# Prompt attention: values of head pairs on two column halves, divided by spread reciprocals

## The reference, cut to what matters

```python
sc = jnp.einsum('bqhd,bqkhd->bqhk', q, kg).astype(jnp.float32) * (q.shape[-1] ** -0.5)
sc = jnp.where(valid[:, :, None, :], sc, -jnp.inf)
p = jax.nn.softmax(sc, axis=-1).astype(v.dtype)
return jnp.einsum('bqhk,bqkhd->bqhd', p, vg)
```

## Time and profile before

| | |
|---|---|
| median of three runs | 2633.05 us |
| the profiled execution | 2633.2 us, span 2631.5 us |
| busy PE / DVE / ACT / POOL | 2504.1 / 1316.3 / 986.7 / 510.4 us |
| prompt attention, first score to last value | 1267.21 to 1593.60 us of the span |

### The profile page before, as it was taken

One profiled execution on the slowest core, in us unless ns is written; L12 is line 12 of the kernel. 1 busy time (PEld: TensorE's weight loads), 2 busy tenths in 40 slices (PEclk: granted clock), 3 DMA queues, 4 the chain that ended last, 5 costly groups with the idle time before them and its releaser, 6 DMA issues. The chain is left out here.

```text
span 2631.5 us, 41101 instructions
## 1 busy us (share of the span) xinstructions
PE 2504.1 (95%) x17116; PEld 2270.4 (86%) x17116; DVE 1316.3 (50%) x2297; ACT 986.7 (37%) x1671; POOL 510.4 (19%) x369
## 2 busy tenths in 40 slices
PE   6999999999998999998799998798999999999997
PEld 6999999988887889997687776477999999988886
DVE  6433333234554379897677764434633333334454
ACT  6333332333432232324566654423433333323332
POOL 0234343400000112382000001000343333310000
PEclk9999999999998999999999999999999999999999
DMA  3122222266552123132202136741122222245553
GB/s 128 51 84 67 85 67 83 75 228 218 199 191 85 35 69 103 35 103 93 83 25 72 59 129 217 271 169 49 51 67 85 67 85 67 84 162 205 202 212 115
DMA packets 153112, 294.34 MB, mean 112 GB/s; under 512 B 14032, under 2 KB 90456, under 8 KB 152928
## 3 DMA queue, kind: packets, MB, share of 16 engines
q1 hardware_dynamic: 146688, 268.12, 29.9%
q0 software_dynamic: 6240, 23.59, 2.5%
HBM read 237.26 MB, written 61.78 MB: 114 GB/s over the span
## 5 line engine op out<-in xcount | busy, mean ns | idle before, releaser
L819 DVE TENSOR_TENSOR f_dl<-f_raw_d,f_dh 128x2048 fp32r<-128x2048 f32 x66 | 151.3, 2293 | 273.7 <-ACT f_dh L634 273.7
L634 ACT ACTIVATE f_dh<-f_raw_d 128x2048 fp32r<-128x2048 f32 x66 | 126.5, 1916 | 321.2 <-PE f_pV L151 286.6
L584 ACT ACTIVATE f_gh<-f_pX 128x256 f32<-128x256 f32 x120 | 49.2, 410 | 311.8 <-PE f_pX L151 311.8
L151 PE MATMUL f_pX<-f_xop,f_u_slo 128*128 128x256 f32 x504 | 149.2, 296 | 0.0
L150 PE MATMUL f_pX<-f_xop,f_u_shi 128*128 128x256 f32 x504 | 149.2, 296 | 0.0
L149 PE MATMUL f_pX<-f_xop,f_u_shi 128*128 128x256 f32 x504 | 149.2, 296 | 0.0
L149 PE MATMUL w_pw<-i_hi,r_T_hi 128*128 128x256 f32 (+1 forms) x504 | 145.3, 288 | 2.6 <-PEq L367 2.6
L2014 ACT ACTIVATE t_sc<-t_sc,t_small 128x640 f32<-128x640 f32 (+8 forms) x136 | 100.0, 735 | 122.1 <-DVE t_small L1943 110.0
L150 PE MATMUL w_pw<-i_lo,r_T_hi 128*128 128x256 f32 (+1 forms) x504 | 144.8, 287 | 0.0
L151 PE MATMUL w_pw<-i_hi,r_T_lo 128*128 128x256 f32 (+1 forms) x504 | 144.2, 286 | 0.0
L584 ACT ACTIVATE f_tu<-f_pX 128x256 f32<-128x256 f32 x126 | 51.7, 410 | 244.5 <-PE f_pX L151 244.5
(11 more groups left out here) (377 smaller groups left out, 8135.8 us busy)
## 6 DMA issues: line engine op xcount, KB each, us to landing
f_raw_d<-in_ffn_w_down SPq DMA_DIRECT2D x66, 1024.0 KB, 5.0
hid<-f_gh SPq DMA_DIRECT2D x22, 1152.0 KB, 9.2
f_raw_h<-hid SPq DMA_DIRECT2D x66, 384.0 KB, 5.5
f_u_raw<-in_ffn_w_up SPq DMA_DIRECT2D x21, 1024.0 KB, 6.4
f_g_raw<-in_ffn_w_gate SPq DMA_DIRECT2D x20, 1024.0 KB, 5.3
proj<-w_stage POOLq DMA_DIRECT2D x12, 1152.0 KB, 5.6
i_raw<-in_w_in SPq DMA_DIRECT2D x12, 1024.0 KB, 5.1
f_x<-in_x_prompt SPq DMA_DIRECT2D x16, 512.0 KB, 6.7
```

Of the source, the lines that this page charges most:

```text
L151: return pe.matmul(out, a[1], b[0], start=False, stop=last, skip_group_check=goes_on)
L584: act.activation(dst, by_tile(pX[:, c, 0:N[c]]), ACT.Copy).then_inc(s_copy, 1)
L634: act.activation(d_hi[slot(q)][:], raw_d[slot(q)][:], ACT.Copy).then_inc(s_dhi, 1)
L819: dve.tensor_tensor(d_lo[slot(q)][:], raw_d[slot(q)][:], d_hi[slot(q)][:].bitcast(F32), ALU.subtract)
```

## The change

Values are taken for two heads at once. The values (128 keys by 64 columns) become stationary, head 2i on the left half of the array's columns and head 2i+1 on the right half, and the turned probabilities (128 by 128) move; the two halves alternate block by block. So the product comes out turned already: columns by queries, two heads above each other in `po`. The row sums lie along the other axis then, so *out* now turns the reciprocals: PE multiplies each head's reciprocal column, repeated 64 times, with the identity, into `pm`; ACT copies that to `osb[:, 0]`, DVE multiplies `po` with it into `osb[:, 1]`. A new step *split* rounds `osb[:, 1]` into `oT_hi` (ACT) and `oT_lo` (DVE).

The plan of a pair becomes: turn 2i, (at head 0 *out* of the tile before,) value of heads 2i-2 and 2i-1, score 2i+2; then turn 2i+1, score 2i+3. *Split* stands at head 2. ACT may fill `pT` of a head when the pair before it is done.

```diff
         plan.append(("turn", g))
+        if h == 0 and g:
+            plan.append(("out",) + tiles[n - 1])
+        if h % 2 == 0 and g:
+            plan.append(("value", g - 2))
         if g + 2 < len(heads):
             plan.append(("score", g + 2))
         if h == 1 and n + 1 < len(tiles):
             plan.append(("keys",) + tiles[n + 1])
-        if g >= 1:
-            plan.append(("value", g - 1))
         if h == 2 and n >= 1:
-            plan.append(("out",) + tiles[n - 1])
+            plan.append(("split",) + tiles[n - 1])
...
-    plan += [("value", len(heads) - 1), ("out",) + tiles[-1]]
+    plan += [("out",) + tiles[-1], ("value", len(heads) - 2), ("split",) + tiles[-1]]
...
 # VectorE
-                elif e[0] == "value" and heads[e[1]][2] == H - 1:
+                elif e[0] == "value" and heads[e[1]][2] == H - 2:
                     n = e[1] // H
-                    dve.wait_ge(s_o, e[1] + 1)
-                    dve_out(dve, None, n)
+                    dve.wait_ge(s_o, H * (n + 1))
+                    dve.wait_ge(s_ma, misc[("o",) + tiles_of[n]] + 1)
+                    dve.tensor_tensor(osb[:, 1, :], po[:], osb[:, 0, :], ALU.mult).then_inc(s_os, 1)
                 elif e[0] == "out":
...
+                    dve.wait_ge(s_p, H * (n + 1))
...
+                    dve.reciprocal(rec[:, n % 2, :], sums[:, n % 2, :]).then_inc(s_rc, 1)
+                elif e[0] == "split":
...
+                    dve.wait_ge(s_oh, n + 1)
+                    dve.tensor_tensor(oT_lo[:, fs, ts], osb[:, 1, :].rearrange("p (f c) -> p f c", c=P),
                                       oT_hi[:, fs, ts].bitcast(F32), ALU.subtract)
...
 # ScalarE (and the one copy of VectorE)
                             if e[1] >= 2:
-                                act.wait_ge(s_o, e[1] - 1)
+                                act.wait_ge(s_o, e[1] // 2 * 2)
...
                 elif e[0] == "out":
                     m = misc[("o",) + e[1:]]
                     act.wait_ge(s_mf, m + 1)
+                    if e[1] * NP + e[2]:
+                        act.wait_ge(s_os, e[1] * NP + e[2])
+                    act.activation(osb[:, 0, :], pm[:], ACT.Copy).then_inc(s_ma, 1)
+                elif e[0] == "split":
+                    act.wait_ge(s_os, e[1] * NP + e[2] + 1)
                     act.activation(oT_hi[:, e[1] * HT:(e[1] + 1) * HT, e[2] * P:(e[2] + 1) * P],
-                                   pm[:].rearrange("p (f c) -> p f c", c=P), ACT.Copy).then_inc(s_ma, 1)
+                                   osb[:, 1, :].rearrange("p (f c) -> p f c", c=P), ACT.Copy).then_inc(s_oh, 1)
...
 # TensorE
-                    for u, _, _ in units[g]:
+                    for u, _, _ in units[g] + units[g + 1]:
                         wait_turned(pe, u)
                     for j in range(nb):
-                        last = pe.matmul(po[:, h * HD:(h + 1) * HD], pT[:, g % 2, j * P:(j + 1) * P],
-                                         v[x][:, k0 + j, h * HD:(h + 1) * HD], start=j == 0, stop=j == nb - 1)
-                    last.then_inc(s_o, 1)
+                        for r in range(2):
+                            last = pe.matmul(po[r * HD:(r + 1) * HD, h * HD:(h + 2) * HD], v[x][:, k0 + j, (h + r) * HD:(h + r + 1) * HD],
+                                             pT[:, (g + r) % 2, j * P:(j + 1) * P], start=j == 0, stop=j == nb - 1)
+                    last.then_inc(s_o, 2)
...
-                    pe.wait_ge(s_os, n + 1)
-                    pe_rows(pe, ("o",) + e[1:], osb[:, n % 2, :])
+                    pe.wait_ge(s_rc, n + 1)
+                    out = pe_misc(pe, ("o",) + e[1:])
+                    for h in range(H):
+                        r, cs = h % 2, slice(h // 2 * P, (h // 2 + 1) * P)
+                        last = pe.matmul(out[r * HD:(r + 1) * HD, cs], rec[:, n % 2, h:h + 1].broadcast_to([P, HD]), ident[:],
+                                         start=True, stop=True)
+                    last.then_inc(s_mf, 1)
```

More of the change, by code:

```diff
@@ L1701, in attn_phase @@
         s_o, s_rc, s_os = sem("value_done"), sem("reciprocal"), sem("out_scaled")
+        s_oh = sem("out_high")
         s_kt = sem("new_keys_placed")
@@ L1751, in attn_phase @@
             elif e[0] == "out":
-                order += [(("o",) + e[1:], 1)]
+                order += [(("o",) + e[1:], 0)]
             elif e[0] == "late":
@@ L1892, in diag @@
             return bass.AP(a.tensor, a.offset + r * DEC_S, [list(a.ap[0]), [PAIR, HT], [1, DEC_S]])
[L1894 to L1901, removed]
         tiles_of = [(x, t) for x in range(2) for t in range(NP)]
@@ L1955, in _ @@
                             if e[1] >= 2:
-                                dve.wait_ge(s_o, e[1] - 1)
+                                dve.wait_ge(s_o, e[1] // 2 * 2)
                             dve.tensor_copy(pT[:, e[1] % 2, b0 * P:(b0 + nb) * P], pt[u % 2][:, 0:nb * P]).then_inc(s_pt[1], 1)
-                elif e[0] == "value" and heads[e[1]][2] == H - 1:
+                elif e[0] == "value" and heads[e[1]][2] == H - 2:
                     n = e[1] // H
-                    dve.wait_ge(s_o, e[1] + 1)
-                    dve_out(dve, None, n)
+                    dve.wait_ge(s_o, H * (n + 1))
+                    dve.wait_ge(s_ma, misc[("o",) + tiles_of[n]] + 1)
+                    dve.tensor_tensor(osb[:, 1, :], po[:], osb[:, 0, :], ALU.mult).then_inc(s_os, 1)
                 elif e[0] == "out":
-                    m = misc[("o",) + e[1:]]
+                    n = e[1] * NP + e[2]
+                    dve.wait_ge(s_p, H * (n + 1))
+                    if n >= 2:
+                        dve.wait_ge(s_mf, misc[("o",) + tiles_of[n - 2]] + 1)
+                    dve.reciprocal(rec[:, n % 2, :], sums[:, n % 2, :]).then_inc(s_rc, 1)
+                elif e[0] == "split":
+                    n = e[1] * NP + e[2]
                     ts = slice(e[2] * P, (e[2] + 1) * P)
-                    dve.wait_ge(s_ma, m + 1)
                     fs = slice(e[1] * HT, (e[1] + 1) * HT)
-                    dve.tensor_tensor(oT_lo[:, fs, ts], pm[:].rearrange("p (f c) -> p f c", c=P),
-                                      oT_hi[:, fs, ts].bitcast(F32), ALU.subtract).then_inc(s_ml, 1)
+                    dve.wait_ge(s_oh, n + 1)
+                    dve.tensor_tensor(oT_lo[:, fs, ts], osb[:, 1, :].rearrange("p (f c) -> p f c", c=P),
+                                      oT_hi[:, fs, ts].bitcast(F32), ALU.subtract)
             dve.wait_ge(s_mask, 1)
```

## The result

The changed kernel takes 2677.49 us, the median of four runs (2675.07 to 2679.3), beside 2633.34 for the kernel before (2632.14 to 2634.14): a ratio of 1.0168 with a 95% interval of 1.0156 to 1.018. It is 44 us slower; 23 were forecast.

What follows compares the result with a forecast made beforehand. PE, 95% busy, bounded the kernel; the change would expose the chain through DVE and ACT. Pairs 293.6 plus tile ends 56.8 minus 1 give 349.4 against 326.4 us: +23, so 2656, range 2639 to 2688 (2622 to 2690 with most cheap ends).

Steps and rivals of the forecast that it cites:

- one mechanism: Prompt attention: with values moved, PE's 1.64 us of work cannot cover the 2.52 us score-to-turn chain; +23 us, chance 0.70.
- A round of two records 0.11, a visit 0.24: Value matmuls on PE: two half-column records share a 0.11 us round; each visit adds 0.24, so 1.34 at five blocks.
- the halves take turns: Rival for the value matmuls: each record still costs 0.106 us, adding 54 us, 2710 in all; chance 0.08.
- The pair's cycle, 5.49 at five blocks: Two heads in prompt attention: chain 2.52, turn 0.55, value 1.34, score 1.08 us, against 5.40 before.
- Cycle by n: Pair times for one to eight key blocks, 1.93 to 7.85 us; four pairs a tile sum to 293.6 us.
- The key and query transposes cost nothing: Transposes fall into PE's 0.9 us wait; ACT's query copies could cost up to 0.85 but were taken at 0.
- The tile end, 3.91: Extra per five-block tile end: 3.91 us from reciprocal wait, `out`, late product and rounding; 56.8 us over the stage.
- the reciprocal's wait: Tile end: PE's `out` waits 1.63 us for DVE's reciprocal, which stands behind reductions and selection steps.
- the late product: Tile end: DVE's product waits for value and ACT's copies, making the next reduction 0.92 us late.
- The clock, priced at nothing: PE's clock could fall with its idle time; the granted clock was expected to stay 1.00, costing 0.
- a PE without gaps at 2595: Rival: PE stays the bound as ACT and DVE keep up; -38 us, 2595 in all; chance 0.09.
- cheap tile ends at 2613: Rival: cycles hold, but DVE's selection steps finish before the reciprocal; ends cost 0.9 to 2.2 us, 2613 at 0.9; chance 0.13.

Runs made afterwards that it cites:

- group A: Not defined in the text; the short query copies cited with it: changed kernel, ACT's two query copies per tile cut to one column, 2673.7 us, ratio 1.0158.

## Why the prediction was right, and where its size failed

The forecast was slower by 23 us from one mechanism, and the mechanism is shown: the order alone, without halves, costs 52 us; with the chain covered again the same halves win 24. The size was half of what came. The forecast's stage is 293.6 + 56.8 = 350.4; measured, from the first score at 1266.99 to the sample's first transposes at 1637.82, it is 370.8. Step by step:

- *A round of two records 0.11, a visit 0.24:* right. From 1400.28 to 1401.52 the 20 records take 1.24, ten rounds of 0.11 and 0.13 for leaving; entering took 0.12 (the turn of 1399.61 streams 0.55). That the halves take turns is refuted. The weight loads of the same 20 records run beside them, within the 1.24:

```profile
1400.28 1.07 PEld L2168 LDWEIGHTS t_po<-t_pT,a_v 128*64 128x64 f32 x20 [0.17 <-issue]
```

By the rule weighed from the Trainium skill, "TensorE: Matmul & The Clock Gate", section Part 3: Packing small matmuls — row/col tiling, each record would have added its weight load. The trace disagrees: 0.11 a round holds no added load.
- *The pair's cycle, 5.49 at five blocks:* 0.22 short. The score behind the values starts the reduction 1.38 after its own start (1401.52 to 1402.90) against 1.28 in the earlier trace rows, and PE's matmul starts 0.72 after the copy's start (1404.60 to 1405.32), where I had 0.63: the copy takes its 0.58, but PE then needs 0.14 instead of the 0.05 of the earlier trace rows. Why is not shown. The earlier trace rows has the weight load alone, but the matmul of the kernel before started with it:

```profile
1275.37 0.43 PE L2161 MATMUL t_po<-a_v,t_pT 128*128 128x64 f32 x2 [0.83 <-ACT t_pT L2050]
```

At six to eight blocks the pairs are 6.48, 7.26 and 8.05, again 0.2 over. For one to four blocks the plain pairs of group A, taken where the short query copies left them free, are 2.3, 3.1, 3.6 and 4.4 against 1.93, 2.70, 3.49 and 4.26. Summed as in the forecast, 4 x (2 x 13.4 + 5 x 5.71 + 21.8) = 309 instead of 293.6: +15 us, the largest error. It is the term "Cycle by n", mis-sized: 7 of the 15 lie at five blocks and more and come from the two later starts, paid in every pair; what makes the 8 at one to four blocks was not told apart.
- *The key and query transposes cost nothing:* 3.8 us for the queries' copies, by the run with short ones; the transposes themselves were not tried.
- *Not foreseen:* the clash of the late item with the keys in `pm`, 6.2 us by the run that moved it. The item stands in the same place in the kernel before, but there PE had a head's values (from 1502.69) between the key transposes of 1501.20 and the item, and stood idle 0.91 ahead of it instead of 4.28. Those values too are cover that the change took away; how much of the 6.2 they explain was not tried:

```profile
1505.15 0.63 PE L2118 MATMUL t_pm<-r_ident,t_srow 128*128 128x128 f32 x4 [0.91 <-issue]
```

- *The tile end, 3.91:* about right in sum, too dear at five blocks. What is left of 370.8 after 309, 3.8 and 6.2 is 52, or 3.5 a tile, against 56.8. At five blocks, for which the forecast worked it out, it is 25.70 - 4 x 5.71 = 2.9: the reciprocal's wait was 0.66 and not 1.63, and 0.75 of the late product was the copies' wait for the values, by the third buffer. So a steady tile of five blocks met its forecast by luck: 25.70 (6.23 + 5.71 + 7.35 + 6.41) against 4 x 5.49 + 3.91 = 25.87, one term too small and the other too large. The shares of the 52 are worked out, not measured one by one.
- *The clock, priced at nothing:* failed; where it was read it cost up to 3.2 us. Table by stretches of the changed kernel, and the `out` matmuls at 1414.00, which lasted 1.09 at 1386.72:

```profile
1411.00:1414.00 3.00, 0.74 (x6) 0.53 (x6) 2.94 (x6) 1.03 (x3) 0.00 (x0) 1.00 0.00 0
1414.00:1417.00 3.00, 3.00 (x30) 3.00 (x32) 0.00 (x0) 0.00 (x0) 0.00 (x0) 0.55 0.00 0
```
```profile
1414.00 1.74 PE L2186 MATMUL t_pm<-r_ident,t_rec 128*64 128x128 f32 x16 [2.17 <-DVE t_rec L1962]
```

PE had been busy 0.74 of 3.00 us; then the granted clock was 0.55, for most of the stretch the 1.2 GHz level. The two pairs there took 9.53 and 7.47 against 7.35 and 6.41 in the tile before, 3.2 in all, part of it the longer wait for the reciprocal. Three such falls lie in the stage behind its first 9 us, none in the kernel before; what they cost in sum was not told apart.
- *The rivals:* a PE without gaps at 2595, halves in turn at 2710 and cheap tile ends at 2613 are all out: plain pairs have gaps of 0.9, rounds last 0.11, and the tile ends cost 2.9 at five blocks and 3.5 on average, above the 2.2 at which the change would be even.

## What to carry to other kernels

An operation that is shortened or moved on the bounding engine is also the cover of the chains beside it: before a saving is booked, add up the work that stands between a chain's start and the instruction that waits for its end, in the new order, with buffers as they then come free. An entry of a shared list moves the work of every engine that reads it, as the reciprocal behind *out* showed. And a reordering and a buffer can each bring little alone (here 8 or 9 us, by an estimate) and much together (46): with either one missing PE still waited once in every pair of five blocks.

## What was not expected of the hardware

A restart of PE behind a wait is not free, and not always the same: 0.14 us from the end of a copy of 0.58 to the first matmul (1404.60 to 1405.32), against 0.05 in the row of the kernel before. The reduction of a score directly behind values on halves started 0.1 later after the score's start than behind a turn (1.38 against 1.28). And idle time of about 2 us on PE, where it was busy for a quarter of a stretch, was followed by a stretch at a granted clock of 0.55.
